# Each engine's own hand-written list of finer steps, in a new order, for two transformer blocks on one core

## Time and profile before

| | |
|---|---|
| Time, median of 3 runs | 917.64 us (916.88 to 918.05) |
| The profiled execution's own time | 917.58 us |
| Its span | 915.8 us |
| TensorE busy, matmuls | 884.1 us, 5660 |
| DVE busy | 655.2 us (72%) |
| ACT busy | 494.4 us (54%) |
| POOL busy | 42.9 us (5%) |
| Weights loaded by SP, 512 KB each | 256, 4.1 us each to landing |
| DMA traffic | 155.06 MB, 169 GB/s over the span |

### The profile page before, as it was taken

How to read it: one execution, slowest core, us unless ns; L and a number is a source line. 1 busy time by engine, 2 the same in 40 slices (tenths; PEclk the granted TensorE clock), 3 DMA queues, 4 the chain that set the end, 5 groups by cost and what they waited for, 6 DMA issues and landing times.

```text
span 915.8 us, 14527 instructions
## 1 busy us (share of the span) xinstructions
PE 884.1 (97%) x5660; PEld 764.8 (84%) x5660; DVE 655.2 (72%) x1190; ACT 494.4 (54%) x898; POOL 42.9 (5%) x72
## 2 busy tenths in 40 slices
PE   8999999999999999899999999999998999999997
PEld 8998988788977888676888888878996788888885
DVE  4769686755767658788787767785657778677676
ACT  5464474565775557655655445535655465444541
POOL 1005000200001100001000000000000100000000
PEclk9999999999999999999999999999998999999999
DMA  8844534374354652123565565545342456565551
GB/s 308 314 163 151 184 116 147 119 241 155 122 184 161 237 189 89 69 70 110 195 220 187 188 204 188 184 159 208 132 145 82 144 189 218 196 205 179 183 191 47
DMA packets 45505, 155.06 MB, mean 169 GB/s; under 512 B 5405, under 2 KB 8061, under 8 KB 45437
## 3 DMA queue, kind: packets, MB, share of 16 engines
q1 hardware_dynamic: 40688, 141.78, 44.9%
q10 hardware_dynamic: 4748, 12.36, 4.3%
HBM read 152.78 MB, written 1.34 MB: 168 GB/s over the span
## 4 chain that ended last, share of the span: by engine, by line
PE 82%; DVE 11%; ACT 3%; issue 1%; DMA 1%; POOL 0%; DVEq 0%; ACTq 0%; SPq 0%
PE ps L2042 15%; PE ps L2066 13%; PE ps L2045 8%; PE ps L785 7%; PE ps L666 6%; PE ps L670 6%; PE ps L667 6%; DVE wlo L633 3%; PE ps L689 3%; PE ps L692 3%; PE ps L686 3%; PE ps L877 3%; PE ps L929 2%; PE ps L886 2%; ACT whi L627 1%
## 5 line engine op out<-in xcount | busy, mean ns | idle before, releaser
L633 DVE TENSOR_TENSOR wlo<-raw,whi 128x1024 fp32r<-128x1024 f32 (+1 forms) x263 | 314.3, 1218 | 41.2 <-ACT whi L627 40.6
L627 ACT ACTIVATE whi<-raw 128x1024 fp32r<-128x1024 f32 (+1 forms) x263 | 271.6, 1047 | 92.8 <-DMA raw<-in_ws 39.6
L2042 PE MATMUL ps<-t,whi 128*128 128x512 f32 x640 | 160.0, 392 | 0.6 <-DVE arena L2160 0.6
L2042 PEld LDWEIGHTS ps<-t,whi 128*128 128x128 f32 x640 | 116.2, 189 | 22.3 <-issue 0.8
L666 PE MATMUL ps<-t,whi 128*128 128x256 f32 (+1 forms) x480 | 120.7, 289 | 0.3 <-ACT arena L1674 0.3
L667 PE MATMUL ps<-t,whi 128*128 128x256 f32 (+1 forms) x480 | 117.5, 283 | 0.0
L666 PEld LDWEIGHTS ps<-t,whi 128*128 128x128 f32 (+1 forms) x480 | 91.2, 190 | 5.6 <-issue 3.9
L2066 PE MATMUL ps<-whi,r 128*128 128x512 f32 x352 | 95.2, 390 | 0.0
L2045 PEld LDWEIGHTS ps<-t,wlo 128*128 128x128 f32 x640 | 87.3, 190 | 6.3
L667 PEld LDWEIGHTS ps<-t,whi 128*128 128x128 f32 (+1 forms) x480 | 91.4, 190 | 0.3
L2045 PE MATMUL ps<-t,wlo 128*128 128x256 f32 x640 | 89.2, 282 | 0.0
(11 more groups left out here) (267 smaller groups left out, 1223.0 us busy)
## 6 DMA issues: line engine op xcount, KB each, us to landing
raw<-in_ws SPq DMA_DIRECT2D x256, 512.0 KB, 4.1
vecs<-in_vecs ACTq DMA_DIRECT2D x12, 512.0 KB, 6.5
arena<-in_ws ACTq DMA_DIRECT2D x5, 512.0 KB, 5.3
raw<-in_ws SPq DMA_DIRECT2D x4, 384.0 KB, 3.2
tb<-brow ACTq DMA_DIRECT2D x8, 192.0 KB, 5.1
rows<-in_mem SPq DMA_DIRECT2D x2, 512.0 KB, 4.4
x<-in_x SPq DMA_DIRECT2D x1, 1024.0 KB, 10.3
rows<-in_ws ACTq DMA_DIRECT2D x2, 512.0 KB, 3.7
```

Source lines behind the costliest of these rows:

```text
L627: a.i.activation(whi[:, j % NSPLIT, 0:n], raw[:, j % NRAW, 0:n], ACT.Copy).then_inc(*a.sig("hi", u))
L633: d.i.tensor_tensor(wlo[:, j % NSPLIT, 0:n], raw[:, j % NRAW, 0:n], whi[:, j % NSPLIT, 0:n].bitcast(F), ALU.subtract).then_inc(*d.sig("lo" ...
L2042: p.i.matmul(ps[:, b, :], wh[:, k, :], t2[:, k, :], start=k == 0, stop=False)
```

## The change

The lists of the stages go. `ORDER[stage][engine]` holds a list for every stage and each of PE, ACT, DVE and POOL, and `steps()` walks it. An engine's order no longer follows from PE's. The steps become finer:

- `tile` / `tlow`, `chunk` / `clow`, `proj` / `plow`, `up` / `ulow`: the two high passes and the low pass are steps of their own, with other steps between them.
- `hi n` and `lo n`: the next n splits of weights, placed by hand, up to six in a row; `AHEAD`, `held`, `due` and `unit_of` go.
- `T k q b`, `turn g s`: halves of transposes. `mask g s`, `exp g s`: a side at a time. `sq`, `gain`, `row`, `xw`, `bn`, `agg`, `cen`, `wr`, `addx s q z`, `seed l q z`: halves of a norm and of the addition of x.
- `KEEP = {}`. pe_warm issues the same number of matmuls on a tile that DVE fills with ones, so it waits for no DMA.
- The transfers on ACT's queue (`vec`, `tbl`, `w1load`) are placed by hand; tables 4 to 7 stand at the end of the odd stage. SP's loads keep their order.
- ALPHA * x is added after fixed numbers of projection units (`ADD_AT`), and other PE steps stand between a product and the addition that follows it.

The arithmetic and the shapes of all products are the same. The diff, cut to its core:

```diff
-AHEAD = NSPLIT - 2
-KEEP = {
-    ("chunk", "o_lora", 0): 4, ("T", 3, 1, 0): 5, ("chunk", "o_lora", 1): 3, ("T", 5, 1, 0): 4, ("chunk", "a_v", 1): 5,
-}
+ORDER = dict(
+    start=dict(
+        pe=listed("""
+        warm 16 7, T 0 0 0, T 0 0 1, T 0 1 0, T 0 1 1, warm 16 3, tile mk0 0, tlow mk0 0, tile mk0 1, tlow mk0 1, tile mk1 0, tile mk1 1,
...
+    even=dict(
+        pe=listed("""
...
+        plow e 3 1, proj e 4 1, proj e 5 1, proj e 6 1, plow e 4 1, plow e 5 1, plow e 6 1, T 3 0 0, proj e 7 1, T 3 0 1"""),
+        act=listed("""
...
+        out d2, hi 2, mix e 2, mix e 3, hi 4, sq post0 0 0, sq post0 0 1, hi 1, sq pre1 0 0, sq pre1 0 1, hi 2, T 3 0 0, sq post0 1 0,
+        sq post0 1 1, hi 1, T 3 0 1, sq pre1 1 0, sq pre1 1 1, hi 1, brow"""),
...
+    odd=dict(
+        pe=listed("""
+        chunk o_lora 0 0, clow o_lora 0 0, chunk o_lora 1 0, clow o_lora 1 0, chunk o_v 0 0, chunk o_lora 2 0, chunk o_lora 3 0,
+        clow o_lora 2 0, clow o_lora 3 0, T 3 1 0, chunk o_v 1 0, T 3 1 1, chunk o_lora 0 1, clow o_lora 0 1, chunk o_lora 1 1, l2 0,
...
+    nsa=dict(
+        pe=listed("""
...
+        tile a_q 4, comp3, tlow a_q 4, val m1, turn n0 0, turn n0 1, tile a_q 5, tlow a_q 5, log n3, turn n1 0, turn n1 1, cmp, log n4,
+        proj a 0 1, turn n2 0, proj a 0 0, plow a 0 0, proj a 1 0, proj a 1 1, cmpt 0, turn n2 1, plow a 0 1, val n0, log n5, turn n3 0,
...
+    moba=dict(
+        pe=listed("""
...
+        proj b 0 1, plow b 2 0, val g4, turn g5 0, proj b 1 1, turn g5 1, plow b 0 1, plow b 1 1, turn g6 0, turn g6 1, val g5,
+        proj b 2 1, plow b 2 1, proj b 3 0, plow b 3 0, proj b 4 0, val g6, plow b 4 0, proj b 5 0, proj b 6 0, plow b 5 0, plow b 6 0,
...
+        dve=listed("""
...
+        pt g3, mul g4, outlo g2, lo 1, outlo g3, mask g5 0, mask g5 1, pt g4, mask g6 0, mask g6 1, mul g5, mul g6, pt g5, outlo g4,
+        addx b 1 0, addx b 1 1, addx b 0 0, addx b 0 1, outlo g5, pt g6, lo 2, outlo g6, lo 2, bn b 0 0, bn b 0 1, agg b 0, cen b 0 0,
...
+    ffn1=dict(
+        pe=listed("""
...
+        up 1 3 3, ulow 1 3 3, up 1 4 0, down 1 1 0 0, down 1 1 1 0, down 1 1 0 1, down 1 1 1 1, ulow 1 4 0, up 1 4 1, ulow 1 4 1,
...
+KEEP = {}
...
+    def steps(section, engine):
+
+        for step in ORDER[section][engine]:
+            yield [step[0]] + [named.get(w, w) for w in step[1:]]
...
-    def act_split(a, upto):
-        for u in due(a, upto):
+    def act_split(a, n):
+
+        for u in split_units[a.split:a.split + n]:
...
     def pe_warm(p, n, bank):
+
         p.fill(bank)
-        for _ in range(2 * n):
-            p.i.matmul(ps[:, bank, 0:P], ident[:, :], ident[:, :], start=True, stop=True)
+        p.wait_ge("ones", 0)
+        for _ in range(n):
+            p.i.matmul(ps[:, bank, 0:P], pt[:, 0, 0:P], pt[:, 0, 0:P], start=True, stop=True)
...
-    def dve_add_x(d, s, q):
+    def dve_add_x(d, s, q, z):
...
```

More of the change, by code:

```diff
@@ L580, in _build @@
-    ADD_AT = {}
-    for steps in (NSA, MOBA):
-        for k, (what, *a) in enumerate(steps):
-            if what == "add_x":
-                ADD_AT[a[0], a[1]] = 1 + max(c[2] for c in steps[:k] if c[0] == "proj" and c[3] == a[1])
+    named = dict(zip("d0 d1 d2 l0 l1 l2 x0 x1 x2 m0 m1 n0 n1 n2 n3 n4 n5 n6 n7 n8 m2 m3 g2 g3 g4 g5 g6".split(),
+                     dsa + mla + diff + mem0 + nsa + mem1 + moba))
+    def steps(section, engine):
+        for step in ORDER[section][engine]:
+            yield [step[0]] + [named.get(w, w) for w in step[1:]]
@@ L743, in pe_mix @@
     def pe_mix(p, s, i):
+        for q in range(2):
+            p.wait_ge("gated", s, q)
         p.fill(6, ("mix_lo", s, i))
@@ L1447, in dve_even @@
         mask = [E["dmask"][:, 0:128], E["dmask"][:, 128:384]]
[L1448 to L1454 removed]
+        for what, *a in steps("even", "dve"):
+            if what == "iw":
                 d.wait_ge("iwT", 0)
@@ L1615, in act_odd @@
-    def act_odd(a):
-        for what, *k in ODD:
-            w = unit_of(what, k)
-            if w:
-                act_split(a, ahead(*w))
-            if what == "T":
-                act_rows_t(a, *k)
-                if k[1] == 1:
-                    a.wait_ge("gained", "post0", 1, 1)
-                    act_vec(a, 3)
-                    a.wait_ge("hrow", "pre1", 1, 1)
-                    act_vec(a, 4)
-            elif what == "tile" and k[0] != "o_kr":
+                    mm = p.i.matmul(ps[:, b, :], l2lo[:, 2, c], wh[:, 0, 512:1024], start=False, stop=True)
@@ L1628, in act_odd @@
+                mm.then_inc(*p.sig("lin", "o_ukv", i))
+            else:
+                pe_common(p, what, a)
+    def act_odd(a):
+        for what, *k in steps("odd", "act"):
+            if what == "tile":
                 name, t = k
@@ L1797, in pe_nsa @@
                 mm.then_inc(*p.sig("w1", u))
[L1798 removed]
+            elif what == "comp1":
                 p.wait_ge("hidr", 0)
@@ L2025, in pe_ffn @@
+    def pe_ffn(p, l):
+        for what, *a in steps(f"ffn{l}", "pe"):
+            if what == "jt":
                 p.fill(6, ("apad_lo", l, 0))
@@ new lines, in pool_ffn @@
+    def pool_ffn(g, l):
+        for what, *k in steps(f"ffn{l}", "pool"):
+            if what == "pad":
+                g.wait_ge("xw", "ab"[l], 1, 1)
+                g.i.memset(FFN["apad"], 0.0).then_inc(*g.sig("pad", l))
+            elif what == "ln":
+                pool_layer_norm(g, *k)
+    def pe_moba(p):
+        for what, *a in steps("moba", "pe"):
+            pe_common(p, what, a)
+    def act_moba(a):
+        for what, *k in steps("moba", "act"):
+            if what == "tile":
```

1637 lines of the change are left out of this document (790 added, 847 removed), and 4 rows, old and new, of the table ODD.

## The result

The kernel after takes 880.88 us in the median (879.64 to 881.73), the one before 917.26 beside it: a ratio of 0.9603 (95% interval 0.9586 to 0.962), 36.4 us less. The prediction said 903.0 with a range of 893 to 914. The direction was right; the size was missed by 22 us, beyond the rival with the largest gain (892).

The account below looks back on a forecast made before the run. TensorE, busy 97% of the span, was taken as the bound, with its idle time, useless work and lower clock to win. Gains of 19.7 us less 5.2 of new waits and FFN losses gave 917.6 - 14.5 = 903, range 893 to 914.

Parts of the forecast that it names:

- difference: Odd stage: projections between the turns of the difference remove two waits for its softmax, 2.0 us.
- norm and o_v: Even to odd mixer: norm halves placed earlier and o_v passes put among o_lora's win 3.8 us.
- compressed softmax: NSA: four projection steps and a turn cover TensorE's 2.6 us wait for DVE's compressed softmax, winning 2.3 us.
- The bound: Whole kernel: only TensorE's 31.7 us of idle time, its useless work and its time at lower clock can be won.
- The new waits: Whole kernel: just-in-time steps and bursts of splits cost 5.2 us, three low-half waits (3.7) plus 1.5 in the FFNs.
- Rival 2: Whole kernel: all idle time but start, tail and 2 us goes, giving 892 us; chance 0.12.
- Idle time "about 20": Sign of being right: TensorE's idle share falls from 31.7 to about 20 us.
- some 8 us less: Sign of being right: TensorE's busy time falls by 4.6 us of idle matmuls and 3.4 of clock.
- Layer b: MoBA: covering the addition of x wins 2.4 us of wait, 3.4 of clock and 1.0 of small waits, 6.8 in all.
- The FFNs: Both FFN stages: nothing to win; later low passes hold split slots longer, priced at 1.5 us lost.
- Rival 4: FFNs: split rings starve as low passes hold slots, 1.22 us lost in each of 20 periods, 926 us; chance 0.14.
- Start: First 40 us: warm-up without waiting for the identity from DRAM wins 1.2 us.

Follow-up runs that it names:

- Run 10: Kernel after with 80 short waits put into the FFNs, each up step's seventh matmul waiting for a POOL memset its fourth releases: median 886.37 us.
- run 2: Kernel before with only the early warm-up, on a tile of ones that DVE fills instead of the identity: ratio 0.9996.
- run 1: Kernel before with KEEP emptied, so the 42 idle matmul instructions are left out and nothing else: ratio 1.0016.
- run 9: Kernel after with the turns of g6 and values of g5 put back behind layer b's unit 2 projection, uncovering the addition of x: 883.43 us.
- run 6: Kernel after with low passes joined outside the FFNs and weight splits in NSA and MoBA tied to TensorE's step again: 906.58 us.
- run 8: Kernel after with the 42 idle matmul instructions put back before the same five steps: 884.11 us.
- run 3: Kernel before with only layer b's list changed: both turns of g6 and values of g5 moved to where x is added: ratio 0.9981.
- item 11: Kernel after with named moves put back one by one: ratios 0.9623 (norm), 0.9628 (o_v), 0.9636 (difference), 0.9666 (softmax).

## Why the prediction was wrong

Three terms make up the miss. The gains were priced at 19.7: 8.0 of busy time (idle matmuls and clock) and 11.7 of idle time. From these 5.2 of new waits were taken off. Measured were 8.1 for the idle matmuls and the clock, as forecast, 20.6 of shown idle time with all new waits in it (8.9 over the 11.7), and 8.0 of hidden waits. The miss of the span is 8.9 + 8.0 + 5.2 = 22.1 us.

- **The small waits, 8.9.** This step failed: I removed the waits that a move of mine explained and left the others. The list named 23 groups; after the change six are left. Shown idle time between the first matmul and the last is 3.8 us, old and new, where it was 22.9. The named moves were sized well where they were tested: difference 2.2 (2 priced), norm and o_v 2.4 (3.8 with the idle matmuls), compressed softmax 2.6 as a wait (2.3).
- **The bound, 8.0.** "What can be won is TensorE's idle time, 915.8 - 884.1 = 31.7 us, the time in which it works on nothing useful, and the time it works at the lower clock." This left out waits under the drawn ends of matmuls. Run 10 shows that such waits exist and are not drawn; the intervals between starts give 8.1 for the two kernels, 5.2 of it in front of shown waits.
- **The new waits, 5.2.** "Against them stand new waits" failed entirely. No wait for a low half is left, and the splits wait for raw data (ACT, 31.3 us in 31 waits) without holding TensorE.
- **Rival 2** is what happened, and it had 0.12: nearly all idle time goes. It left 2 us between the ends where 3.8 are left. With the two terms that its sum lacks, the idle matmuls (4.7) and the hidden waits (8.0), its 892 becomes 879.6.
- **A slip in the signs.** Idle time "about 20" and busy time "some 8 us less" add up to 19.7, the gains without the new waits. They do not belong to the 14.5 of the forecast.
- **Layer b.** 6.8 predicted, 9.9 measured in its stretch. The clock's 3.4 and the wait's 2.5 went as said. The 3.4 was in part luck: it is the fall of one profiled execution, and the profiles of runs 2 and 1 show 1.7 and nothing in that place. The cause was only half right: the cover alone wins 1.1 to 1.8 (run 9), and the larger part of the stretch is low passes apart and the placing of the splits (run 6). What the Trainium skill says, that only longer gaps let the clock fall (TensorE: Matmul & The Clock Gate, "Why this matters for your kernels"), is not borne out: the falls of eight traces stand behind waits of 1.9 to 2.6 us (a ninth has three, behind 2.6 to 3.1). But no such gap is sure to bring one.
- **The FFNs.** "Nothing to win", -1.5. The stretches with them gained 1.3 and 2.3 us, 2.1 of it idle time that the trace before shows at their two ends and not inside, the rest hidden. Rival 4 (the split rings starve) found no row.
- **Start.** 1.2 by itself is 0 (run 2); with the whole of the order the kernel is 4.1 ahead by T 3, for 2.0 priced.
- **Right:** direction, no wait for the addition, no wait for the compressed softmax, a clock of 1.00 in MoBA, FFN windows full. That work takes the idle matmuls' place is right in part (run 8).

What stays open: of odd's 11.2 us the moves undone one by one account for 4.6 and the idle matmuls for some 1.5 (run 8); the rest was not taken apart, nor were the waits of even. In NSA and MoBA the whole is split by kind of change (run 6), not by wait. The finer steps of ACT and DVE (halves of masks, norms and the addition) were nowhere undone by themselves.

## What to carry to other kernels

When an engine is 97% busy by a profile that draws its instructions longer than their issue interval, look at the intervals between starts as well as at its idle time: here 31.7 us of idle time stood beside some 8 us of gain that it did not contain. An order of steps for several engines is one object. Low passes apart lost 10 us in the old order and won 12 in the new one; the new lists with joined passes outside the FFNs and tied splits in two stages won 11 of the 36 (906.6 us against 917.4); all together won 36. So judge such a change by how many small waits it can reach and not by the few it can be seen to reach. In this case a wait list with some twenty small entries and no long one was one that a full reordering could nearly clear.

## What the runs showed of the hardware that was not expected

The clock's fall is not tied to one gap. In the kernel before, waits of 2.6 (softmax) and 2.5 us (addition) stand 327 us apart; the profiled execution fell to 0.50 behind the second for 6.8 us, run 2 behind the second for 3.4, and run 3, where the second was gone, behind the first for 3.4. Without the idle matmuls it fell twice, for 3.4 and 10.2 us, behind waits of 1.7 us and less, and then behind neither of the two long ones; the mean clock of all ten executions of that kernel lies at or below the lowest of the kernel before. Nor does it need a gap: in the runs of the norm and the softmax of item 11 it fell at 352 us, behind this group, with no idle time shown for 12 us before (timeline of the norm's run: begin, duration, instruction):

```profile
349.11 2.76 PE L1922 MATMUL ps<-arena 128*128 128x32 f32 x24
```

These 24 matmuls have 32 columns each. In the kernel after, in two profiled executions, the same group and waits of up to 1.3 us brought no fall before the tail. Such a place is a chance of losing 1.7 to 5.1 us, and a single execution doesn't tell whether it will.
